# Window-attention values projected feature-major and transposed, with the first query projection freed of a wait

## The chip, the cores and the metric

The kernel runs on one core of one Trainium2 chip. The metric is the device time of one launch in microseconds (us), the median over runs. TensorE is called PE here, its weight loads PEld, VectorE DVE, ScalarE ACT, GpSimd POOL, and SP is the engine that issues the weight loads from memory.

## The reference

Two transformer-like blocks are computed one after the other on 512 latent tokens and 256 context tokens with 1024 features. The change is in the second block, which has two layers. Each layer normalises and modulates its tokens to `u`, projects them, runs three attention branches (latent-rank, differential, and local with a window), merges them with gates, and ends in a convolutional feed-forward part. The local branch is the one that changes:

```python
def window_gqa(c_lat, c_ctx, cos, sin, sink, ctx_queries):
    q, k, v = heads(*c_lat)          # 8 query heads, 2 key/value heads of 64
    cq, ck, cv = heads(*c_ctx)
    q = apply_rope(q, cos, sin)
    k = apply_rope(k, cos, sin)
    ...
        s_c = jnp.einsum('bqgrd,bkgd->bgrqk', qn, ck, ...) * scale
        s_b = jnp.einsum('bqgrd,bkgd->bgrqk', qn, kn, ...) * scale
        s_b = jnp.where(ok, s_b, NEG_INF)
        p = softmax_with_sink(jnp.concatenate([s_c, s_b], axis=-1), sink_b)
        return (jnp.einsum('bgrqk,bkgd->bqgrd', p[..., :n_ctx], cv)
                + jnp.einsum('bgrqk,bkgd->bqgrd', p[..., n_ctx:], vn))
```

Keys and values are projected from all 768 tokens, so the value matrix has 768 tokens by 128 features (two heads of 64). Layer 0 also computes the context's queries, layer 1 does not (`ctx_queries`).

## The kernel before, in words

The program is one straight line of instructions for each engine, written out by Python functions named `..._pe`, `..._act`, `..._dve`, `..._pool`. There is no loop on the chip; the order on an engine is the order in which these functions are called, and the engines meet at semaphores. Weights come as tiles of up to 128 x 2048 numbers. For each tile SP starts the load into one of four `raw` buffers once the matmuls of the tile four places earlier are done (`fill_raw`, line 177 issues it), ACT rounds it to `high` (line 203), DVE subtracts to get `low` (line 218), and PE takes both (`take`). Activations `U` are kept feature-major (features on partitions, 768 tokens along the columns) as the same kind of pair.

A product is three matmuls for each 128 features of the contraction, high by high, high by low and low by high, so 24 for a contraction of 1024 (`product`, line 269). Which operand streams through PE is chosen in two ways:

- `project`: the weights are loaded, the tokens stream. The result is feature-major, and each matmul has 512 columns (the latents) or 256 (the context).
- `token_major`: 128 tokens of `U` are loaded, the weight columns stream. The result has tokens on partitions. For n = 128 value features each matmul has 128 columns, and there are six tiles of tokens:

```python
def token_major(k, out_of, tile, c0, n, U, kcs, inc_of):
    per = 512 // n
    for i in range(0, 6, per):
        b = out_of(i // per)
        for j, t in enumerate(range(i, min(i + per, 6))):
            ins = product(k.pe, b[:, j * n:(j + 1) * n], ...)
```

PSUM is eight banks of 128 x 512 numbers `B[0]` to `B[7]`, and also four pairs of them, `W[0]` (banks 0 and 1) to `W[3]` (banks 6 and 7).

The window branch of a layer comes third, behind the merge of the differential branch. `window_keys_pe` takes the tile `wkv`, projects k with `project` into B[2] and B[3], projects v with `token_major` into B[4] and B[5], and multiplies k by the rotation matrix into B[6] (`rope_pe`, line 2740, plain float32, two records in the trace). `A.enter_pe` and `A.enter2_pe` wait until the merge before has read the banks. ACT copies k (line 2733) and v (line 2766) out. DVE and POOL finish the rotary embedding of k: POOL multiplies k by the cosines (line 2757), DVE the product by the sines (line 2747), and DVE adds them (line 2750), which gives the event `roped`.

`attention_pe` follows. It first issues the pieces of query group 0 (`window_pieces`: `q0`, the projection of 512 latents; `rq`, its rotation; `q1`, the projection of 256 context tokens, in layer 0 only). The code of `q0` holds a wait ahead of its first matmul:

```python
        if g == 0:
            pe.wait_ge("roped", (tag, "k"))
            pe.wait_ge("loaded", (tag, "v"))
```

ACT copies q out (line 3147), PE rotates it (line 3640), DVE and POOL finish it (lines 3275, 3285, 3278). Then 16 or 24 steps follow (four query groups by four or six blocks of 128 queries): scores (line 2963), mask and maximum on DVE (lines 2986, 2989, 2992), exponential on ACT (line 3007, where the first one also loads a table), normalising, transposition of the weights on PE into W[3] (line 3057), copy out on ACT (line 3064), and the product with v (line 3084). `H.ready_pe` lets the scores of a group start only when k, q and v are all loaded and k and q are rotated. Group 1 and later query pieces are issued in the gaps of these steps. `A.P` are the buffers of the exponentials; the first is written by the first exponential.

## Time and profile before

| what | value |
|---|---|
| median of 3 runs | 5345.15 us (5344.71 to 5349.12) |
| span of the profiled execution, first to last instruction | 5338.9 us |
| its own time around that span | not listed apart; the fastest run is 5.8 us longer than the span, the median 6.3 us |
| instructions | 67117 |
| busy: PE, PEld, DVE, ACT, POOL | 92%, 78%, 58%, 36%, 23% of the span |
| mean granted TensorE clock | 0.968 |
| layer 0, window branch: first k matmul to first scores | 3216.20 to 3256.63 us |
| layer 1, the same | 4691.99 to 4731.05 us |

The span is cut into its stages by the last two lines. A stage of one engine is read from the starts of its instructions, since matmuls overlap: a row's duration is longer than the distance to the next start.

### The profile page before, as it was taken

Reading aid. Unit: us, or ns where it says so; the run is one execution under the profiler, and the core shown is the slowest. Engines: PE = TensorE matmul, PEld = TensorE weight load, DVE = VectorE, ACT = ScalarE, POOL = GpSimd, SP = SyncE. Lnnn points to the kernel's source line nnn. Section 1 sums busy time; section 2 is a strip of 40 time slices with the busy share of each in tenths; the row PEclk is TensorE's granted clock in tenths of the full one; section 3 lists DMA queues with packets and bytes.
Section 4 is the critical chain, followed back from the end, with each engine's and each line's share of the span. In section 5 each row is a group of like instructions: output and inputs, shape, how many; then the busy total and the mean of one; then the engine's idle time right before and its main releaser. Section 6 shows DMA issues by size and latency. Waiting matters only on the chain.

```text
span 5338.9 us, 67117 instructions
## 1 busy us (share of the span) xinstructions
PE 4931.0 (92%) x27321; PEld 4145.3 (78%) x27321; DVE 3090.8 (58%) x5380; ACT 1910.7 (36%) x2848; POOL 1212.2 (23%) x1009
## 2 busy tenths in 40 slices
PE   7998999998899999989899999999999899889999
PEld 7887878787688878878668777778888677667787
DVE  4544456689657777776542534456666544454555
ACT  3445422235732222223342424322322443343332
POOL 1111000047644555543120002100000120021000
PEclk8999999999999999999899999999999999999999
DMA  4111124422568888875101011122322101112222
GB/s 155 49 52 57 40 80 141 158 89 111 213 247 295 306 304 307 318 283 192 52 14 68 24 40 34 44 95 101 113 103 103 50 28 65 37 52 95 87 92 74
DMA packets 157154, 636.29 MB, mean 119 GB/s; under 512 B 12352, under 2 KB 62544, under 8 KB 106288
## 3 DMA queue, kind: packets, MB, share of 16 engines
q1 hardware_dynamic: 112528, 467.97, 24.3%
q0 software_dynamic: 42240, 160.88, 8.4%
q8 instruction: 218, 3.57, 0.3%
q10 hardware_dynamic: 2080, 3.15, 0.2%
q14 instruction: 88, 0.72, 0.0%
HBM read 595.25 MB, written 36.70 MB: 118 GB/s over the span
## 4 chain that ended last, share of the span: by engine, by line
PE 64%; DVE 15%; ACT 7%; POOL 6%; issue 4%; DMA 4%; SPq 0%; DVEq 0%; ACTq 0%; POOLq 0%
PE banks L269 51%; ACT high L203 2%; DVE low L218 2%; PE banks L2958 2%; POOL ownv L2339 2%; PE banks L2963 2%; DVE ownu L2349 1%; DVE cols L2989 1%; POOL ge L2490 1%; PE banks L3057 1%; DVE oa L2275 1%; ACT P L3007 1%; PE banks L3084 1%; DMA raw<-uT_in 1%; PE banks L1022 1%
## 5 line engine op out<-in xcount | busy, mean ns | idle before, releaser
L218 DVE TENSOR_TENSOR low<-raw,high 128x2048 fp32r<-128x2048 f32 (+2 forms) x333 | 730.3, 2194 | 797.7 <-ACT high L203 775.3
L269 PE MATMUL banks<-UH,high 128*128 128x512 f32 (+2 forms) x2784 | 1016.9, 365 | 44.8 <-DVE UL L510 12.5
L269 PE MATMUL banks<-UL,high 128*128 128x512 f32 (+2 forms) x2784 | 1004.0, 361 | 0.0
L269 PE MATMUL banks<-UH,low 128*128 128x512 f32 (+2 forms) x2784 | 1002.8, 360 | 0.0
L203 ACT ACTIVATE high<-raw 128x2048 fp32r<-128x2048 f32 (+3 forms) x341 | 617.3, 1816 | 762.1 <-DMA raw<-uT_in 272.6
L269 PEld LDWEIGHTS banks<-UH,high 128*128 128x128 f32 (+1 forms) x2784 | 526.3, 189 | 146.3 <-issue 40.6
L269 PEld LDWEIGHTS banks<-UH,low 128*128 128x128 f32 (+1 forms) x2784 | 526.8, 189 | 86.3
L269 PEld LDWEIGHTS banks<-UL,high 128*128 128x128 f32 (+1 forms) x2784 | 526.6, 189 | 82.8 <-issue 0.7
L269 PE MATMUL banks<-UpH,high 128*128 128x384 f32 (+1 forms) x1152 | 404.7, 351 | 58.0 <-issue 29.5
L269 PE MATMUL banks<-UpH,low 128*128 128x384 f32 (+1 forms) x1152 | 400.7, 348 | 0.0
L269 PE MATMUL banks<-UpL,high 128*128 128x384 f32 (+1 forms) x1152 | 400.5, 348 | 0.0
L269 PE MATMUL banks<-high,actH 128*128 128x512 f32 x768 | 306.1, 399 | 29.1 <-issue 16.9
L269 PE MATMUL banks<-low,actH 128*128 128x512 f32 x768 | 303.6, 395 | 0.0
L269 PE MATMUL banks<-high,actL 128*128 128x512 f32 x768 | 303.5, 395 | 0.0
L2989 DVE TENSOR_REDUCE cols<-banks 128x1 f32<-128x768 f32 (+3 forms) x240 | 190.6, 794 | 187.1 <-PE banks L2963 107.4
L269 PEld LDWEIGHTS banks<-UpH,high 128*128 128x128 f32 x1152 | 221.3, 192 | 77.3 <-issue 70.5
L4160 POOL TENSOR_TENSOR cv<-cv 128x768 f32<-128x768 f32 (+1 forms) x44 | 68.9, 1566 | 844.3 <-DVE cv L4120 844.3
L2334 POOL DMA_INDIRECT ownu<-un_in,ownat x128 | 166.0, 1297 | 341.4 <-DVE ownu L2349 326.3
L2456 ACT ACTIVATE actH<-ge 128x384 fp32r<-128x384 f32 x128 | 67.3, 526 | 467.4 <-POOL ge L2490 463.9
L3007 ACT ACTIVATE P<-banks,cols 128x768 f32<-128x768 f32 (+3 forms) x240 | 184.7, 772 | 124.5 <-DVE cols L2994 97.3
L269 PEld LDWEIGHTS banks<-UpL,high 128*128 128x128 f32 x1152 | 221.5, 192 | 6.4
L269 PEld LDWEIGHTS banks<-UpH,low 128*128 128x128 f32 x1152 | 220.9, 192 | 5.9
(423 smaller groups left out, 9981.4 us busy)
## 6 DMA issues: line engine op xcount, KB each, us to landing
raw<-uT_in SPq DMA_DIRECT2D x64, 1024.0 KB
raw<-ev_in SPq DMA_DIRECT2D x64, 1024.0 KB
raw<-up_in SPq DMA_DIRECT2D x44, 1024.0 KB
raw<-ada_in SPq DMA_DIRECT2D x40, 1024.0 KB
gd<-stage SPq DMA_DIRECT2D x12, 2048.0 KB, 6.6
gt<-gd SPq DMA_DIRECT2D x32, 768.0 KB, 5.8
side<-ada_in SPq DMA_DIRECT2D x24, 1024.0 KB, 5.0
raw<-gate_in SPq DMA_DIRECT2D x24, 1024.0 KB
```

The lines of the kernel that those rows point to most:

```text
L203: a.e.activation(k.high[i % SPL][:, 0:w], k.raw[j % RAW][:, 0:w], ACT.Copy).then_inc(*a.inc("w_hi", j))
L218: v.e.tensor_tensor(k.low[j % RAW][:, 0:w], k.raw[j % RAW][:, 0:w], k.high[i % SPL][:, 0:w].bitcast(F32), ALU.subtract).then_inc(*v.inc("w ...
L269: ins = pe.e.matmul(out, x, y, start=start and i == 0 and j == 0, stop=stop and i == n - 1 and j == 2)
L1022: ins = pe.e.matmul(o[:, c * 64:(c + 1) * 64], w.S[:, c, x * 128:(x + 1) * 128], w.qd[:, c * 64:(c + 1) * 64], start=False, stop=(c == ord ...
L2334: g.e.indirect_dma_start(S.u[s % NUB][:], None, k.dram["un"], bass.IndirectOffsetOnAxis(S.at[:, s:s + 1], 0)).then_inc(*g.inc(f"own_u{s % ...
L2339: g.e.indirect_dma_start(S.v[s % NVB][:], None, k.dram["vn"], bass.IndirectOffsetOnAxis(S.at[:, s:s + 1], 0)).then_inc(*g.inc(f"own_v{s % ...
L2456: a.e.activation(k.acts[n % 2].h[:, i, :], k.ge[i][:], ACT.Copy).then_inc(*a.inc("act_hi", (n, i)))
L2958: ins = pe.e.matmul(k.W[1 + j][:, at:at + n], Q[lo:hi, q * 128:(q + 1) * 128], K[lo:hi, k0:k0 + n], start=True, stop=True)
L2963: ins = pe.e.matmul(k.W[1 + jj][:, at:at + n], Q[lo:hi, q * 128:(q + 1) * 128], K[lo:hi, k0:k0 + n], start=True, stop=True)
L2989: v.e.reduce_max(mx, src, AX_X).then_inc(*v.inc("largest", (tag, i, j)))
L3007: a.e.activation(A.P[i % 2][j][:, 0:width], src, ACT.Exp, bias=nb, scale=A.scale, accum_out=r).then_inc(*a.inc("exp", (tag, i, j)))
L4160: g.e.tensor_tensor(va[:, 0:w], va[:, 0:w], ga[:, 0:w], ALU.mult).then_inc(*g.inc("ffn_prod", (l, j)))
```

## The change

The function `values_act` is removed. `window_keys_pe` projects v like k, with `project`: weights loaded, tokens streaming, 512 and then 256 columns, into the same banks B[4] and B[5]. ACT copies that feature-major result to `A.vT`, which is the memory of the first exponential buffer `A.P[0][0]`. The rotation of k goes to B[0] instead of B[6]. The wait ahead of the first `q0` matmul is gone. Behind the 24 matmuls of the first `q0`, `window_values_pe` transposes vT in six blocks of 128 x 128 into W[3], and `window_values_act` copies all 768 columns to `A.v` in one instruction, behind ACT's copy of that `q0`. All this is done once in each of the two layers.

```diff
@@ window_plan
     A.plan(k)
+    A.vT = A.P[0][0]
@@ window_keys_pe
-    token_major(k, lambda i: B[4 + i], tile, 128, 128, k.U, KC,
-                lambda i: pe.inc("mm", ((tag, "v"), i), *([("tile", tile.j)] if i else [])))
+    for r, region in enumerate(BOTH):
+        project(k, B[4 + r][:, 0:region[1]], tile, KC, 128, k.U, region).then_inc(
+            *pe.inc("mm", ((tag, "vT"), r), *([("tile", tile.j)] if r else [])))
     A.enter2_pe()
-    rope_pe(k, A.k, 128, k.r64, B[6], (tag, "k"))
+    rope_pe(k, A.k, 128, k.r64, B[0], (tag, "k"))
+
+def window_values_pe(k, A):
+    pe, tag = k.pe, A.tag
+    pe.wait_ge("loaded", (tag, "vT"))
+    for t in range(6):
+        ins = pe.e.transpose(k.W[3][:, t * 128:(t + 1) * 128], A.vT[:, t * 128:(t + 1) * 128], k.ident[:])
+    ins.then_inc(*pe.inc("mm", (tag, "v")))
@@ window_keys_act
-    values_act(k, A.v, 128, (B[4], B[5]), (tag, "v"))
+    to_sbuf_act(k, (B[4], B[5]), BOTH, A.vT, 128, (tag, "vT"), (tag, "vT"))
     a.wait_ge("sinks", A.l)
+
+def window_values_act(k, A):
+    a, tag = k.act, A.tag
+    a.wait_ge("mm", (tag, "v"))
+    a.e.activation(A.v[:], k.W[3][:, 0:T].rearrange("p (t n) -> p t n", n=128), ACT.Copy).then_inc(*a.inc("loaded", (tag, "v")))
@@ window_keys_dve
-    rope_dve(k, A, A.k, 128, k.B[6], (A.tag, "k"))
+    rope_dve(k, A, A.k, 128, k.B[0], (A.tag, "k"))
@@ window_piece_pe
-        if g == 0:
-            pe.wait_ge("roped", (tag, "k"))
-            pe.wait_ge("loaded", (tag, "v"))
...
         if u == of - 1:
             ins.then_inc(*pe.inc("mm", (tag, w, g), *([("tile", A.tile.j)] if last else [])))
+            if g == 0 and p == 0:
+                window_values_pe(k, A)
@@ window_piece_act
         load_act(k, A, bank, n, 128, A.qs[g % 2][:, c0:c0 + n], ((tag, w, g), (tag, "q", g)), (tag, w, g))
+        if g == 0 and p == 0:
+            window_values_act(k, A)
```

The order moves at three places, shown for layer 0; layer 1 has the same without the `q1` piece. In the names, `high` and `low` are the two parts of a weight tile, `UH` and `UL` those of the activations, and `banks0` to `banks3` stand for W[0] to W[3].

PE, the end of the value projection, the rotation of k and the start of the first `q0`, before:

```order
L269 MATMUL banks2<-high0_57,UH_305 128x128
L269 MATMUL banks2<-low3_56,UH_305 128x128
L269 MATMUL banks2<-high0_57,UL_306 128x128
L2740 MATMUL banks3<-k_385,r64_303 128x512 [waits loaded,branch]
L269 MATMUL banks0<-UH_305,high1_58 128x512 [waits roped,loaded,w_lo,w_hi]
```

and with the change:

```order
L269 MATMUL banks2<-UH_305,high0_57 128x256
L269 MATMUL banks2<-UL_306,high0_57 128x256
L269 MATMUL banks2<-UH_305,low3_56 128x256
L2740 MATMUL banks0<-k_385,r64_303 128x512 [waits loaded,branch]
L269 MATMUL banks0<-UH_305,high1_58 128x512 [waits w_lo,w_hi]
```

The 144 value matmuls of 128 columns have become 24 of 512 and 24 of 256, the rotation of k writes banks0, and the first `q0` matmul waits for its weights only.

PE, the end of that `q0` and what follows it, before:

```order
L269 MATMUL banks0<-UH_305,low0_53 128x512
L3640 MATMUL banks1<-q_387,r64_303 128x512 [waits loaded]
L269 MATMUL banks1<-UH_305,high1_58 128x256
```

and with the change:

```order
L269 MATMUL banks0<-UH_305,low0_53 128x512
L3583 MATMUL banks3<-ident_61,P_393 128x128 [waits loaded]
L3583 MATMUL banks3<-ident_61,P_393 128x128 x5
L3645 MATMUL banks1<-q_387,r64_303 128x512 [waits loaded]
L269 MATMUL banks1<-UH_305,high1_58 128x256
```

The six transpositions stand between the projection and the rotation of q, and have a wait of their own for vT (which bears the name P here, whose memory it is).

ACT, from the copies of k to the first exponential, before:

```order
L2733 ACTIVATE k_385<-banks1 128x256 [waits mm]
L2766 ACTIVATE v_386<-banks2 128x512 [waits mm]
L2766 ACTIVATE v_386<-banks2 128x256 [waits mm]
L203 ACTIVATE high0_57<-raw2_51 128x2048 [waits w_raw2,sinks]
L3147 ACTIVATE q_387<-banks0 128x512 [waits mm]
L3147 ACTIVATE q_387<-banks1 128x256 [waits mm]
L3007 ACT_TABLE_LOAD
```

and with the change:

```order
L2733 ACTIVATE k_385<-banks1 128x256 [waits mm]
L2733 ACTIVATE P_393<-banks2 128x512 [waits mm]
L2733 ACTIVATE P_393<-banks2 128x256 [waits mm]
L203 ACTIVATE high0_57<-raw2_51 128x2048 [waits w_raw2,sinks]
L3137 ACTIVATE q_387<-banks0 128x512 [waits mm]
L3599 ACTIVATE v_386<-banks3 128x768 [waits mm]
L3137 ACTIVATE q_387<-banks1 128x256 [waits mm]
L2997 ACT_TABLE_LOAD
```

ACT has one instruction more, the copy of the transposed values, between the two copies of q. DVE and POOL keep their order.

## Rows read from the trace of the kernel before

**Rows 1.** The page: busy time of the engines, and the chain that ended last by engine

```profile
PE 4931.0 (92%) x27321; PEld 4145.3 (78%) x27321; DVE 3090.8 (58%) x5380; ACT 1910.7 (36%) x2848; POOL 1212.2 (23%) x1009
...
PE 64%; DVE 15%; ACT 7%; POOL 6%; issue 4%; DMA 4%; SPq 0%; DVEq 0%; ACTq 0%; POOLq 0%
```

**Rows 2.** The chain of waits in layer 0, 3180 to 3300: start, us, what

```profile
3240.82 0.93 PE banks L2740 x2
3241.82 1.27 POOL k L2757
...
3243.19 0.70 DVE k L2750
...
3244.13 7.39 PE banks L269 x24
...
3251.55 0.61 ACT q L3147
...
3252.20 1.12 PE banks L3640 x2
...
3256.19 0.39 ACT q L3147
3256.63 1.18 PE banks L2963 x8
```

**Rows 3.** Busy time by stretch in layer 0, columns in its first line

```profile
core 0: us, PE busy (x) PEld busy (x) DVE busy (x) ACT busy (x) POOL busy (x), PEclk, DMA share, GB/s
3216.20:3221.79 5.59, 5.59 (x26) 4.51 (x25) 1.18 (x2) 1.92 (x1) 3.96 (x5) 1.00 0.73 251
3221.79:3224.63 2.84, 2.84 (x25) 2.83 (x24) 2.24 (x2) 0.60 (x1) 0.00 (x0) 1.00 0.41 143
3224.63:3240.66 16.03, 16.03 (x146) 16.03 (x145) 0.00 (x0) 0.98 (x2) 0.00 (x0) 1.00 0.00 1
3240.66:3244.13 3.47, 1.07 (x4) 0.27 (x4) 1.64 (x3) 2.18 (x2) 1.26 (x1) 1.00 0.50 151
3244.13:3251.34 7.21, 7.21 (x24) 5.56 (x24) 1.95 (x1) 0.00 (x0) 0.00 (x0) 0.76 0.00 0
```

**Rows 4.** The same by stretch in layer 1

```profile
4700.42:4716.44 16.02, 16.02 (x146) 16.02 (x145) 0.00 (x0) 0.98 (x2) 0.00 (x0) 1.00 0.00 1
4716.44:4719.92 3.48, 1.08 (x5) 0.28 (x4) 1.65 (x3) 2.18 (x2) 1.26 (x1) 0.92 0.49 151
4719.92:4726.88 6.96, 6.96 (x24) 5.39 (x24) 1.94 (x1) 0.00 (x0) 0.00 (x0) 0.80 0.00 0
4726.88:4731.05 4.17, 1.29 (x4) 0.30 (x3) 1.39 (x2) 1.88 (x2) 1.26 (x1) 1.00 0.00 0
```

**Rows 5.** Timeline of PE in layer 0: start, us, engine, what

```profile
3267.88 0.77 PE L3057 MATMUL banks<-ident,P 128*128 128x128 f32 x5
3268.40 0.48 PE L269 MATMUL banks<-UH,high 128*128 128x512 f32 x1
```

**Rows 6.** Timeline of ACT, a copy in layer 0 and the start of layer 1's queries

```profile
3268.68 0.71 ACT L3064 ACTIVATE PT<-banks 128x640 f32<-128x640 f32 x1 [1.55 <-PE banks L3057]
...
4727.70 1.28 ACT L3007 ACT_TABLE_LOAD   x1
...
4733.52 0.69 ACT L3007 ACTIVATE P<-banks,cols 128x512 f32<-128x512 f32 x1 [4.54 <-DVE cols L2992]
```

**Rows 7.** Timeline of PE in layer 1, rotation of q and first scores

```profile
4727.73 1.12 PE L3640 MATMUL banks<-q,r 128*128 128x512 f32 x2 [0.69 <-ACT q L3147]
4731.05 1.13 PE L2963 MATMUL banks<-k,q 64*128 64x256 f32 x8 [2.19 <-DVE q L3278]
```

**Rows 8.** Busy time by stretch, from the first scores of a layer onward

```profile
3256.63:4691.99 1435.36, 1337.30 (x7749) 1096.37 (x7750) 782.07 (x1312) 482.38 (x743) 167.31 (x108) 0.98 0.20 72
4731.05:4825.00 93.95, 79.77 (x644) 57.44 (x645) 63.08 (x183) 56.73 (x137) 31.39 (x19) 1.00 0.06 18
4731.05:5338.90 607.85, 576.37 (x2766) 456.24 (x2766) 322.17 (x472) 217.46 (x307) 71.03 (x50) 0.99 0.23 79
```

More of the change, by code:

```diff
@@ L2757, in rope_pool @@
     g.e.tensor_tensor(x[0:m, 0:TX], x[0:m, 0:TX], a.C[0:m, :], ALU.mult).then_inc(*g.inc("rope_cos", key))
-def values_act(k, dst, n, banks, key):
-    a = k.act
-    per = 512 // n
-    for i, t in enumerate(range(0, 6, per)):
-        m = min(per, 6 - t)
-        a.wait_ge("mm", (key, i))
-        a.e.activation(dst[:, t:t + m, 0:n], banks[i][:, 0:m * n].rearrange("p (t n) -> p t n", n=n), ACT.Copy).then_inc(
-            *a.inc("loaded", key))
 def key_parts(kind, q):
```

## The prediction

> **What bounds the kernel now.** I read the page first: PE is busy for 92% of the span and holds 64% of the chain that ended last, no other engine more than 15% [rows 1]. So the question is what PE does, and what it waits for, between the first k matmul and the first scores of the window branch in each of the two layers. Nothing outside these two places is edited.
>
> The chain of waits in layer 0 [rows 2] passes through this place without a detour: value projection on PE, rotation of k, the cosine product on POOL, the sum on DVE, then the 24 matmuls of the first q, ACT's copy, the rotation of q, and the first scores. PE therefore stands on the path for all of it except where the chain goes to POOL and DVE, and there it stands idle.
>
> The table by stretch [rows 3, 4] gives what each step takes, from start to start:
> - the k projection in layer 0: 5.59 us for 24 matmuls of 512 columns and 2.84 for 24 of 256, together 8.43, at full clock (2.4 GHz level, 1.00 in the row);
> - the value projection: 16.03 us in layer 0 and 16.02 in layer 1 for 144 matmuls of 128 columns, PE and PEld busy all the time, full clock. That is 0.111 us for one, hardly less than the 2.84 / 24 = 0.118 of one with twice the columns;
> - the rotation of k up to the first q matmul: 3.47 and 3.48 us, of which PE works 1.07 and 1.08 and idles 2.40;
> - the first q, again 24 matmuls of 512 columns: 7.21 and 6.96 us, with a mean granted clock of 0.76 and 0.80. The clock has gone to its lower level (1.2 GHz) behind the idle 2.40 us and comes back within this q. The same 24 matmuls took 5.59 at full clock.
>
> **The change, part by part.** The sum is made on the profiled execution, whose span is 5338.9 us; the median of the runs is 5345.15, so 6.3 us lie around the span or are scatter, and the change doesn't touch them. I subtract the gain from the median.
>
> Value projection: 144 matmuls of 128 columns go, 24 of 512 and 24 of 256 come. These are the k projection's own shapes with the same activations streaming, and both regions are projected in both layers, so the price is its row, 8.43 us. Gain 16.03 - 8.43 = 7.60 in layer 0 and 16.02 - 8.43 = 7.59 in layer 1. All of it is on the path, since PE has nothing else to do there and no one holds it up: the weights of the next two tiles are split long before.
>
> The wait ahead of the first q: 2.40 us idle in each layer [rows 3, 4]. It goes whole, since the remaining condition is the split q weights, which ACT and DVE made during the merge before and at the start of k. POOL and DVE still need 0.93 (PE's rotation) + 1.27 + 0.70 and the hand-overs, from 3240.82 to 3243.89 [rows 2], but now beside the q matmuls (5.59), and only the first scores ask for the result.
>
> The clock in the first q: if PE doesn't idle, the reason for the fall is gone. 7.21 - 5.59 = 1.62 in layer 0 and 6.96 - 5.59 = 1.37 in layer 1. Bounds: nothing, if the clock falls at this place in any case, and these two differences. I take the differences, because in 3216.20 to 3240.66, with no idle time, every row has 1.00.
>
> The six transpositions: the nearest row is the same operation on the exponentials, where five start at 3267.88 and the next matmul at 3268.40 [rows 5], so 0.52 / 5 = 0.104 each and 0.62 for six. They stand where PE waits anyway: ACT's copy of q begins at 3251.55, when the projection has ended, takes 0.61, and the rotation starts at 3252.20 [rows 2]; the last q stretch ended at 3251.34 [rows 3], so 0.86 us lie there. 0.62 fits in, so the cost is 0. From below nothing; from above the row's own duration, 0.77 for five, so about 0.9 in all, would come out by less than 0.1. The ceiling is six times the whole 0.77 - 4 x 0.104 = 0.35 one after the other, 2.1 - 0.86 = 1.3 a layer. I take 0, by the distance between starts, and keep 1.3 for the range.
>
> ACT: the two copies out of B[4] and B[5] have the same sizes as those they replace, 0. The new copy of 768 columns: nearest is 0.71 us for 640 [rows 6], so about 0.85. It starts when the transpositions end, some 0.9 us behind the end of q, and is done at about 1.8. In layer 0 the next thing ACT is wanted for is the copy of q1 at 3256.19 [rows 2], 4.85 us behind that end (3251.34), so 3 us of cover. In layer 1 there is no q1: the first scores, which also wait for the values, start at 4731.05 [rows 7], 4.17 us behind 4726.88, cover 2.4; the table load behind it (1.28 us) moves from 4727.70 to about 1.1 us later, and the first exponential runs at 4733.52 [rows 6], cover more than 3. Cost 0; without that cover it would be 0.85 a layer. Also ahead of the first q copy stands the rounding of the next weight tile, which waits for the end of the value projection. It comes 7.6 us earlier like its release, and has the whole of k's rotation and q (1.07 + 5.59 = 6.66 us) to finish in.
>
> The rotation of k in B[0] instead of B[6], and DVE's sine product there: same size, 0. B[0] is waited for together with B[6], by the same condition. The buffer that vT borrows is first used by the first exponential, which comes behind the scores and so behind the values.
>
> What is late next: in layer 0 the first scores still wait for ACT's copy of q1, in layer 1 for DVE's sum of q (2.19 idle, rows 7). Both run from the rotation of q as before. Every later instruction follows this chain, and each weight tile is fetched when an earlier one is used up, so it moves along; behind the first scores the mean busy share of the DMA engines is 0.20 and 0.23 [rows 8]. The distance is kept to the end.
>
> Sum: layer 0 7.60 + 2.40 + 1.62 = 11.62; layer 1 7.59 + 2.40 + 1.37 = 11.36; together 22.98 us. 5345.15 - 22.98 = 5322.2 us. Its span would be 5315.9.
>
> The Trainium skill speaks against the price of the transpositions: the page "TensorE: Matmul & The Clock Gate", section "Part 4: PE-mode transpose", says that one of 128 x 128 costs about 275 ns inside a kernel, mostly access latency. By that six take 1.65 us, 0.79 more than the gap holds, and the sum would be 1.6 us less, 5323.8. The trace disagrees as to what the path pays: starts are 104 ns apart [rows 5].
>
> **The rivals.**
>
> *The lower clock stays in the first q.* Something else than the idle time brings it down, for instance the plain float32 rotation ahead of it. Against: the clock was 1.00 in the stretch of layer 0 that holds the rotation [rows 3]. For: in layer 1 it was already 0.92 there [rows 4]. Gain 22.98 - 2.99 = 19.99, time 5325.2.
>
> *Only the projection gains.* The wait moves instead of going: PE stands for the rotated k, or for vT, elsewhere ahead of the scores. Needed for it is a chain of over 6 us from the end of the value projection; the one of k is 3.2 (3240.82 to 3243.89 and before it 0.16), ACT's copy of vT is 0.60. Then 15.19 us are left, time 5330.0.
>
> *Given back later.* The instructions gain their 23 us, but a later stage is set by something that doesn't move, such as weight transfers, or the clock falls at new places behind waits. For: behind the first scores of layer 0 the mean clock was 0.98 for 1435 us and 0.99 for 608 [rows 8], so about 2 x 0.02 x 1435 + 2 x 0.01 x 608 = 70 us were spent at the lower level, and each such piece may come or go when all is moved by 12 to 23 us. Against: the three runs, which have the same instructions, lie within 4.4 us. So I count 4.4 us either way, and for more, down to no measurable gain, about 5339.
>
> *Slower: the clock falls at the first scores of layer 1 and stays down through the window steps.* Place: 4726.88 to 4731.05, where PE works 1.29 of 4.17 us and was granted 1.00 nonetheless [rows 4]. With the transpositions in the gap, there is less pure waiting but also hardly more real work. Price: a matmul at the lower level takes up to twice as long, so each us of work at full clock loses up to one. To turn 22.98 us of gain into 10.7 of loss (0.2%) the lower level would have to hold for work that took 34 us at full clock; the decision falls there. The first 94 us of steps hold 79.8 us of PE work at full clock [rows 8] and could lose up to that: 5402. Against: the steps of both layers already have waits of 1 to 2 us in each and recovered.
>
> The same page and section of the Trainium skill say that transpositions do not count as activity for the clock. By that rule the six would leave the gap behind q as idle as before, and this rival would be no less likely than without them. The trace of before has that gap without a fall.
>
> **How the numbers follow.** Chances: the sum with its scatter 0.88, the lower clock in q 0.04, only the projection 0.04, given back to no gain 0.03, slower 0.01. What the measurement can tell from no change is about 0.2%, 10.7 us, so 5334.5 to 5355.8. The first three cases are all faster than that: faster 0.96, same 0.03, slower 0.01. The range: 5322.2 less the 4.4 of scatter, and 1.3 for small gaps that close as well, gives 5316.5; upward it takes in the lower clock, the dear transpositions (2 x 1.3) and the case of the projection alone at 5330.0.
>
> **What the profile afterwards would show.** Right: 96 matmuls fewer in each layer; the value projection in 8.4 us; no idle time between the rotation of k and the first q, and q in 5.6 us at clock 1.00; six transpositions behind it and the rotation of q about 0.86 us behind the end of q, still released by ACT's copy; first k matmul to first scores 28.8 us instead of 40.4 in layer 0 and 27.7 instead of 39.1 in layer 1; the rest from first scores to end as long as before within a few us. Wrong: the value projection at over 9 us; a new wait of PE on ACT's vT or v; q again at 7 us without idle time ahead of it; or the stretch behind the first scores longer by more than 5 us, which would say that the gain was given back.

## The result, and the profile after

| | before | changed |
|---|---|---|
| median, us | 5347.09 (5344.71 to 5349.12, 4 runs) | 5314.55 (5308.57 to 5320.82, 4 runs) |
| ratio, 95% interval | | 0.9942 [0.9931, 0.9954] |
| profiled execution, us | | 5317.05, span 5315.7 |
| first k matmul to first scores, layer 0 / 1 | 40.43 / 39.07 | 28.82 / 27.57 |

The change makes the kernel faster, by 32.5 us in this comparison. The forecast was 5322.2 with a range from 5316.5 to 5330.0, so the median lies 2 us under its low end. The two stages came out as forecast (28.8 and 27.7). What lies between these two facts is what the experiments had to find.

The page of the changed kernel, first its size and busy times, then the chain that ended last by engine:

```profile
span 5315.7 us, 66759 instructions
...
PE 4909.2 (92%) x27141; PEld 4120.8 (78%) x27141; DVE 3092.2 (58%) x5380; ACT 1912.3 (36%) x2850; POOL 1212.0 (23%) x1009
...
PE 62%; DVE 16%; ACT 7%; POOL 6%; DMA 4%; issue 4%; SPq 0%; DVEq 0%; ACTq 0%; POOLq 0%
```

PE still bounds the kernel. Its share of the chain is 62% here and 64% in [rows 1], but other executions of the same two kernels have 62% (before) and 64% and 60% (changed), so this share tells nothing of the change. Busy time by stretch of the changed kernel, with the columns of [rows 3], the places being those of [rows 3, 4, 8]: k projection, value projection, rotation of k to rotation of q, rotation of q to first scores, then the middle; the same for layer 1, then its first scores up to the second ones, and the rest:

```profile
3219.92:3228.36 8.44, 8.44 (x51) 7.36 (x50) 3.42 (x3) 2.52 (x2) 3.95 (x5) 1.00 0.64 214
3228.36:3236.79 8.43, 8.43 (x50) 7.35 (x49) 0.00 (x0) 0.98 (x2) 0.00 (x0) 1.00 0.00 0
3236.79:3244.10 7.31, 7.28 (x35) 5.42 (x33) 3.59 (x3) 2.79 (x3) 1.30 (x1) 1.00 0.23 72
3244.10:3248.74 4.64, 3.96 (x27) 3.31 (x27) 1.39 (x2) 1.43 (x3) 1.29 (x1) 1.00 0.00 0
3248.74:4678.22 1429.48, 1331.28 (x7749) 1092.32 (x7749) 782.33 (x1312) 482.21 (x743) 167.27 (x108) 0.98 0.20 72
4678.22:4686.65 8.43, 8.43 (x50) 7.34 (x49) 3.24 (x4) 2.52 (x2) 4.67 (x6) 1.00 0.59 210
4686.65:4695.08 8.43, 8.43 (x50) 7.34 (x49) 0.00 (x0) 0.98 (x2) 0.00 (x0) 1.00 0.01 2
4695.08:4702.39 7.31, 7.28 (x35) 5.42 (x33) 3.59 (x3) 2.79 (x3) 1.31 (x1) 1.00 0.25 72
4702.39:4705.79 3.40, 1.12 (x2) 0.32 (x3) 1.39 (x2) 2.09 (x2) 1.26 (x1) 1.00 0.00 0
4705.79:4711.44 5.65, 5.65 (x21) 3.96 (x21) 3.23 (x11) 1.93 (x6) 0.00 (x0) 0.70 0.00 0
4705.79:5315.70 609.91, 579.15 (x2766) 456.69 (x2766) 322.26 (x472) 217.33 (x307) 71.01 (x50) 0.98 0.23 79
```

The value projection takes 8.43 us, the price of k's. From the rotation of k to that of q it is 7.31 us with PE busy for 7.28 of them, and the granted clock is 1.00 (the 2.4 GHz level) in both layers. One row is new: at the first scores of layer 1 the mean granted clock is 0.70 and they take 5.65 us. The same stretch of the kernel before:

```profile
4731.05:4735.63 4.58, 4.12 (x21) 2.90 (x21) 3.04 (x9) 1.89 (x6) 0.00 (x0) 1.00 0.00 0
```

So 1.07 us of the gain are given back there. At another place, the last scores of layer 0's window steps, the clock went the other way. From the scores that start 97.94 us behind the first ones to the start of the last group of scores, in the kernel before and then in the changed one:

```profile
3354.57:3375.51 20.94, 17.82 (x129) 12.05 (x129) 13.24 (x42) 11.98 (x35) 6.90 (x4) 0.77 0.00 1
```

```profile
3346.68:3365.67 18.99, 15.33 (x129) 10.63 (x129) 13.24 (x42) 12.08 (x35) 6.90 (x4) 0.91 0.01 2
```

The same instructions take 1.95 us less at a higher granted clock. It is so in every profile of the two kernels: 20.94 and 20.74 us before (0.77 and 0.84), 18.99, 18.88 and 18.72 changed (0.91 each).

The chain of waits of the changed kernel in layer 0, in order of time:

```profile
3236.95 0.86 PE banks L2740 x2
3237.81 5.60 PE banks L269 x24
3243.41 0.66 PE banks L3583 x6
3244.07 0.03 issue
3244.10 1.13 PE banks L3645 x2
3245.22 2.85 PE banks L269 x24
3248.08 0.02 issue
3248.10 0.39 ACT q L3137
3248.49 0.25 issue
3248.74 1.16 PE banks L2953 x8
```

POOL and DVE, which stood in [rows 2] with the rotation of k, are gone. The six transpositions (L3583) fill the gap between the last q matmul and the rotation of q, which begins as soon as ACT's copy of q is done. The timeline of ACT over the same stretch shows that copy, the new copy of the values, and the cover behind it:

```profile
3243.45 0.60 ACT L3137 ACTIVATE q<-banks 128x512 f32<-128x512 f32 x1 [4.27 <-PE banks L269]
3244.10 0.81 ACT L3599 ACTIVATE v<-banks 128x768 f32<-128x768 f32 x1
3248.10 0.38 ACT L3137 ACTIVATE q<-banks 128x256 f32<-128x256 f32 x1 [3.19 <-PE banks L269]
```

The copy of v takes 0.81 us, and ACT then idles 3.19 us. The spans differ by 5338.9 - 5315.7 = 23.2 us: first k matmul of layer 0 3.72 later (3216.20 to 3219.92), stage of layer 0 -11.61, middle -5.87, stage of layer 1 -11.50, rest +2.06. The stages alone give 23.11. The three others nearly cancel, and their instructions are the same in both kernels. The middle holds the 1.95 us gained at the end of layer 0's steps, and the rest the 1.07 us given back at layer 1's first scores.

### The profile page after: what moved, and what is told of

It reads as the page before. It is cut to its first block, busy times and chain, and to the rows that moved or that the text cites. A ratio compares the mean times of both kernels' runs of the same rounds, so it can differ in the third digit from the quotient of the medians.

```text
span 5315.7 us, 66759 instructions
## 1 busy us (share of the span) xinstructions
PE 4909.2 (92%) x27141; PEld 4120.8 (78%) x27141; DVE 3092.2 (58%) x5380; ACT 1912.3 (36%) x2850; POOL 1212.0 (23%) x1009
## 4 chain that ended last, share of the span: by engine, by line
PE 62%; DVE 16%; ACT 7%; POOL 6%; DMA 4%; issue 4%; SPq 0%; DVEq 0%; ACTq 0%; POOLq 0%
PE banks L269 49%; ACT high L203 2%; DVE low L218 2%; DMA raw<-uT_in 2%; PE banks L2948 2%; PE banks L2953 2%; DVE oa L2275 1%; DVE ownu L2349 1%; POOL ownv L2339 1%; POOL ge L2490 1%; PE banks L3047 1%; DVE cols L2979 1%; ACT P L2997 1%; PE banks L3074 1%; PE banks L1022 1%
## 5 line engine op out<-in xcount | busy, mean ns | idle before, releaser
L269 PE MATMUL banks<-UH,high 128*128 128x512 f32 (+2 forms) x2816 | 1028.8, 365 | 39.8 <-DVE UL L510 12.2
```

The lines of the kernel that those rows point to most:

```text
L269: ins = pe.e.matmul(out, x, y, start=start and i == 0 and j == 0, stop=stop and i == n - 1 and j == 2)
```

## The experiments

The first theory: the prediction's mechanism is whole, the stages give 23 us, and the remainder is scatter between executions that lies outside them, around a base that was taken too high. The rival: the change gains or loses elsewhere too, by way of the clock or of the buffers.

All runs in one table. Stages are from the first k matmul to the first scores; the part in brackets is from the rotation of k to that of q. early_q and early_q2 have another order, so there is nothing to put in brackets; a kernel that ran once has no ratio. Each ratio is to runs of the kernel before in the same comparison.

| run | span | ahead of layer 0's k | stage 0 | middle | stage 1 | rest | median of runs, us | ratio to the kernel before |
|---|---|---|---|---|---|---|---|---|
| kernel before | 5338.9 | 3216.20 | 40.43 (11.54) | 1435.35 | 39.07 (11.29) | 607.85 | | |
| before_again | 5332.8 | 3213.10 | 40.42 (11.53) | 1432.07 | 39.23 (11.45) | 607.98 | 5336.78 | 0.9996 [0.9983, 1.0008] |
| changed kernel | 5315.7 | 3219.92 | 28.82 (7.31) | 1429.48 | 27.57 (7.31) | 609.91 | 5314.55 | 0.9942 [0.9931, 0.9954] |
| after_again | 5317.1 | 3218.56 | 28.81 (7.30) | 1433.03 | 27.58 | 609.12 | 5316.34 | 0.9956 [0.9942, 0.9969] |
| after_third | 5309.7 | 3213.85 | 28.82 | 1430.52 | 27.58 | 608.93 | 5315.08 | 0.9953 [0.9939, 0.9966] |
| wait_only | 5332.5 | 3216.79 | 36.30 (7.35) | 1432.59 | 35.24 (7.36) | 611.58 | 5334.92 | 0.9994 [0.9985, 1.0003] |
| values_only | 5316.6 | 3213.66 | 31.25 (9.94) | 1431.59 | 30.21 (10.02) | 609.89 | 5325.38 | 0.9972 [0.9962, 0.9982] |
| values_again | 5322.6 | 3216.55 | 31.23 (9.93) | 1434.02 | 30.21 (10.02) | 610.59 | 5323.86 | |
| idle_back | 5322.3 | 3216.66 | 31.18 (9.82) | 1434.10 | 31.67 (11.39) | 608.69 | 5323.56 | |
| idle_again | 5315.7 | 3217.14 | 31.19 (9.84) | 1427.69 | 31.66 (11.37) | 608.02 | 5317.07 | |
| twelve | 5319.8 | 3220.60 | 29.17 (7.77) | 1433.45 | 27.95 (7.76) | 608.63 | 5321.14 | |
| late_turn | 5323.6 | 3221.64 | 28.81 (7.31) | 1436.25 | 27.58 (7.30) | 609.32 | 5324.97 | |
| early_q | 5317.3 | 3219.58 | 27.78 | 1432.64 | 25.18 | 612.17 | 5321.33 | 0.9962 [0.9948, 0.9975] |
| early_q2 | 5315.2 | 3219.61 | 27.78 | 1433.62 | 25.18 | 608.96 | 5312.70 | 0.9945 [0.9932, 0.9959] |

Stages repeat within 0.02 us for the same instructions and the same clock. The columns around them move by several us even between executions of one kernel (3213.10 and 3216.20 for that of before). So a stage tells apart what a median of a few runs can't.

### The same kernels once more

after_again and after_third are the changed kernel unaltered, before_again is the kernel before.

> The changed kernel once more, five rounds. Two theories for the 32.5 us between the medians, where the steps in the two window stages sum to 23.0. A (scatter): the edit is worth the 23 us of the stages and the rest is the spread of executions, so this run gives a ratio near 0.9957 (23 us less, within 4), and its profile has 28.8 and 27.6 us from the first k matmul to the first scores, with the stretches around them scattering either way. B (a further systematic gain behind the stages, by fewer falls of the clock): a ratio near 0.994 again (30 us or more less), with the stretch from the first scores of layer 0 to the first k matmul of layer 1 at 1429 to 1430 us again, where it was 1435.4.

> The kernel before against itself, five rounds, which shows what the comparison gives for no change. Theory A: ratio 1.000 within 0.0008, and a profile whose stretches outside the window stages differ by several us from the first one's (span between 5335 and 5350). Theory B: ratio 1.000 too, but the stretch between the two stages stays at 1435 within 1 us.

> The changed kernel a third time, five rounds, to see where its ratio settles. If the edit is worth what the stages show (23.1 us less up to the first scores, at most 1.1 given back in layer 1), the ratio is 0.9957 within its interval, and the stages are 28.8 and 27.6 us again while the stretches before, between and behind them move by several us. If the first comparison (0.9942) was the true one, the ratio is at or under 0.9945.

before_again has the ratio 0.9996 [0.9983, 1.0008] to the kernel before, which it is. The stages came out at 28.8 and 27.6 each time, and the middle, 1433.03 and 1430.52 in the changed kernel, was 1432.07 in before_again: theory A, the stages and scatter, holds in the main, and of theory B's gain behind the stages only the 2 us at the end of layer 0's steps are seen again. All runs together give a base that three runs could not: 58 of the kernel before, median 5340.6, from 5329.3 to 5361.1, standard deviation 5.7; 14 of the changed one, median 5315.7, from 5306.8 to 5322.8, standard deviation 4.5. The difference of the medians is 24.9, that of the means 25.0 with a 95% interval of 2.8 either way. The stages' 23.1 lie in it. With the two places where the clock changed, about 1.0 given back and 2.0 gained in the means of the profiles, some 24 us are accounted for. The interval takes the executions as independent. They come from several comparisons, and only 7 of the 54 others of the kernel before are as long as the shortest of the first four, 5344.71, so those four were probably long for a reason beyond this scatter. The four of the changed kernel beside them were not (5314.55, where all 14 have 5315.7). The later comparisons ran on chips 0, 8 and 13, that of the first isn't recorded, and the reason stays open.

Where the spread sits, busy time by stretch: from 2520.00 us to the first k matmul of layer 0, in the kernel before and then in before_again, its second profiled execution.

```profile
2520.00:3216.20 696.20, 629.11 (x3787) 502.81 (x3787) 303.04 (x578) 245.28 (x434) 90.07 (x62) 0.95 0.12 41
```

```profile
2520.00:3213.10 693.10, 625.24 (x3798) 500.96 (x3797) 303.75 (x580) 245.85 (x436) 90.07 (x62) 0.96 0.12 41
```

Nearly the same matmuls (3787 and 3798 records) take 3.10 us longer in the first, and PE is busy 3.87 us longer, at 0.95 granted instead of 0.96. So at least part of the scatter is the length of time for which the clock is down. That it is all of it isn't shown.

### One part of the change alone

wait_only takes the two waits out of the kernel before and leaves the value projection token-major:

```diff
         A.tile = view(take(k, (A.l, "wq", g // 2)), KC)
-        if g == 0:
-            pe.wait_ge("roped", (tag, "k"))
-            pe.wait_ge("loaded", (tag, "v"))
```

> Only the two waits ahead of the first q are taken out; the values stay token-major and there are no transpositions. Theory A: 2 x 2.40 us of idle time and the 2.99 us at the lower clock go, 7.8 us in all, ratio 0.9985; the value projection stays at 16.0 us, q at 5.6 in both layers. Rival, the clock falls in the first q whatever goes before: 4.8 us, and q stays at about 7. Theory B: more than 7.8, by several us.

Busy time by stretch of wait_only: rotation of k to rotation of q in layer 0 and in layer 1, then the first scores of layer 1 up to the second.

```profile
3241.26:3248.61 7.35, 6.66 (x28) 4.75 (x28) 3.59 (x3) 2.79 (x3) 1.30 (x1) 1.00 0.23 71
4710.15:4717.51 7.36, 6.67 (x29) 4.76 (x28) 3.59 (x3) 2.82 (x4) 1.30 (x1) 1.00 0.24 71
4720.92:4727.69 6.77, 6.77 (x21) 4.74 (x21) 3.37 (x11) 1.92 (x6) 0.68 (x1) 0.56 0.00 0
```

11.54 and 11.29 became 7.35 and 7.36, idle time ahead of q and slow clock both gone. The two stages are 4.13 and 3.83 shorter, together 7.96, beside 7.79 forecast (2 x 2.40 + 2.99). But the first scores of layer 1 take 6.77 us at a clock of 0.56 instead of 4.58: 2.19 us come back at once. So 5.8 us net, and the ratio, which should be 0.9989 by that, is 0.9994 [0.9985, 1.0003]: it agrees but does not tell the gain from none.

values_only keeps the waits and transposes directly behind the rotation of k (ACT's copy of the values moves forward with it, and neither stands behind q0 any longer):

```diff
     rope_pe(k, A.k, 128, k.r64, B[0], (tag, "k"))
+    window_values_pe(k, A)
...
+        if g == 0:
+            pe.wait_ge("roped", (tag, "k"))
+            pe.wait_ge("loaded", (tag, "v"))
```

> Only the projection is turned round: values in 512 and 256 columns, transposed directly behind the rotation of k, and the first q waits for the rotated k and the values as before. Theory A: 7.60 + 7.59 = 15.2 us less, ratio 0.9972; the transpositions lie inside the wait (3.47 us from the rotation to the first q stays, idle 1.7 instead of 2.4), and the clock still falls in q, 7 us. Rival, the shorter idle time no longer brings the clock down: 18.2 us. Theory B: more than 15.2 by several us.

> The same kernel as in values_only, one more look. There an idle time of 1.7 us ahead of the first q brought no fall in either layer (9.9 and 10.0 us). If idle time below 2.4 us is short enough, that is so again; if the moment decides, one of the two may be at 11.4.

The same stretches of values_only:

```profile
3230.53:3240.47 9.94, 7.52 (x34) 5.34 (x32) 3.68 (x3) 3.59 (x4) 1.26 (x1) 1.00 0.16 53
4693.37:4703.39 10.02, 7.51 (x34) 5.33 (x32) 3.68 (x3) 3.62 (x5) 1.26 (x1) 1.00 0.18 52
4706.71:4712.33 5.62, 5.62 (x20) 3.81 (x20) 3.36 (x11) 1.92 (x6) 0.00 (x0) 0.70 0.00 0
```

Stages 9.18 and 8.86 shorter, together 18.0, where the projection alone would give 15.19. The other 2.9 are the clock: PE still waits (9.94 - 7.52 = 2.42 us over the whole stretch of layer 0, of which 1.74 ahead of q, 1.83 in layer 1), but the clock stayed at 1.00. It did so again in values_again. The ratio, 0.9972 [0.9962, 0.9982], is 15.0 us of 5340, the stages less the 1.04 at the first scores being 17.0. The ratio is the one expected with the clock falling in q, and the traces show the rival instead; its interval holds both.

The two parts are therefore not additive in the clock term: either of them keeps the clock up in q, so 18.0 + 7.96 = 26.0 counts 2.9 twice, and 23.1 are had by both.

### The idle time put back into the changed kernel

```diff
         A.tile = view(take(k, (A.l, "wq", g // 2)), KC)
+        if g == 0:
+            pe.wait_ge("roped", (tag, "k"))
```

> The changed kernel with one wait put back: the first q waits for the rotated k again (not for the values). If the idle time of 2.40 us is what brings the clock down, rotation of k to rotation of q goes from 7.31 us back to about 11.4 (3.47 + about 7.1 + 0.86) in both layers, stages of 32.9 and 31.7 us. The rival, that the 16 us of 128-column matmuls ahead of it had their part in the fall: the idle time alone comes back, 9.9 us at clock 1.00, stages of 31.4 and 30.2. Where the clock falls in q of layer 1, it should not fall again at the first scores of that layer.

> The same kernel as in idle_back, one more look at the clock. There the same 2.40 us of idle time cost a fall in layer 1 and none in layer 0. If the place in the program decides, it is the same again: 9.8 us from the rotation of k to that of q in layer 0, 11.4 in layer 1. If the moment decides, at least one of the two can be otherwise.

Busy time by stretch of idle_back: the first 3.47 us from the rotation of k, then up to the rotation of q, in layer 0 and in layer 1. The first q matmul starts 3.31 us behind the rotation in both layers, after 2.29 us of idle time, so the first row of each pair ends with 0.16 us of q.

```profile
3233.53:3237.00 3.47, 1.18 (x5) 0.38 (x4) 1.69 (x3) 2.18 (x2) 1.26 (x1) 1.00 0.40 151
3237.00:3243.35 6.35, 6.32 (x30) 4.96 (x30) 1.90 (x1) 0.60 (x1) 0.00 (x0) 1.00 0.00 0
4698.81:4702.28 3.47, 1.18 (x5) 0.38 (x4) 1.70 (x3) 2.18 (x2) 1.26 (x1) 1.00 0.49 151
4702.28:4710.20 7.92, 7.89 (x31) 6.13 (x30) 1.89 (x1) 0.60 (x1) 0.00 (x0) 0.78 0.00 0
```

The whole stretch of idle_again in the two layers:

```profile
3234.01:3243.85 9.84, 7.52 (x35) 5.34 (x33) 3.59 (x3) 2.78 (x3) 1.26 (x1) 1.00 0.16 53
4692.90:4704.27 11.37, 9.05 (x34) 6.50 (x32) 3.59 (x3) 2.78 (x3) 1.26 (x1) 0.85 0.15 46
```

The idle time of some 2.3 us costs itself in both layers. In layer 1 the clock falls, and the second row has 7.92 instead of 6.35 us; in layer 0, behind the same instructions and the same idle time, it doesn't. The second execution gives the same split, so neither the expectation nor its rival came out whole. No run without the idle time had a fall in q (twelve places: two layers of six profiles), so it seems to be needed; it does not suffice, and which place falls is set by something that repeats from run to run. The prediction's "if PE doesn't idle, the reason for the fall is gone" holds; its converse does not. The rival named above, that the 128-column matmuls ahead have a part in the fall, isn't settled: the kernel before, which has them, fell in all four places, idle_back and idle_again, which don't, in two of four.

### The price of the transpositions

twelve makes the six transpositions twice:

```diff
-    for t in range(6):
+    for t in (0, 1, 2, 3, 4, 5, 0, 1, 2, 3, 4, 5):
```

> The changed kernel with each of the six transpositions of the values issued twice (same result). By the distance between starts, 0.104 us each, six more cost 0.62 us: 7.31 becomes 7.9 us from the rotation of k to that of q, in both layers. If each cost 0.27 us on the path, as its own duration has it, 12 would take 3.3 us and the stretch would be 9.9.

```profile
3237.47:3245.24 7.77, 7.77 (x41) 6.15 (x40) 3.59 (x3) 2.79 (x3) 1.31 (x1) 1.00 0.20 67
4700.10:4707.86 7.76, 7.76 (x40) 6.14 (x39) 3.59 (x3) 2.79 (x3) 1.31 (x1) 1.00 0.22 68
```

From the rotation of k to that of q 7.77 instead of 7.31: six more cost 0.46 us. PE has no idle time left there (busy 7.77 of 7.77). The timeline of PE in layer 0 of twelve gives the distance between starts:

```profile
3243.93 1.47 PE L3583 MATMUL banks<-ident,P 128*128 128x128 f32 x12
3245.24 0.59 PE L3645 MATMUL banks<-q,r 128*128 128x512 f32 x1
```

The same in the changed kernel:

```profile
3243.25 0.82 PE L3583 MATMUL banks<-ident,P 128*128 128x128 f32 x6
3244.10 0.70 PE L3645 MATMUL banks<-q,r 128*128 128x512 f32 x1
```

Twelve take 1.31 us from their first start to the rotation of q, 0.109 each where [rows 5] gave 0.104. Six are then 0.65 of the 0.85 us that lie there in the changed kernel, which leaves 0.20, and the 0.46 are the other six less that. By the 275 ns of the Trainium skill ("TensorE: Matmul & The Clock Gate", "Part 4: PE-mode transpose") six more would be 1.65 us. The trace agrees with that figure as the duration of one (0.27 us: 1.47 less eleven times 0.109), but what the path pays is the distance between starts, 0.109.

### Where the transpositions stand in layer 1

late_turn moves them, in layer 1 only, from behind q0 to behind the rotation of q, into PE's wait ahead of the first scores:

```diff
         pe.e.matmul(bank, k.r64[:], A.qs[g % 2][:, 0:TX], start=True, stop=True).then_inc(...)
+        if g == 0 and not A.ctx_out:
+            window_values_pe(k, A)
...
-            if g == 0 and p == 0:
+            if g == 0 and p == 0 and A.ctx_out:
                 window_values_pe(k, A)
```

> In layer 1 alone the six transpositions go behind the rotation of q, into the idle time ahead of the first scores (2.28 us). The stages stay at 28.8 and 27.6 us. If it is that idle time which brings the clock down at the first scores of layer 1, a break of 1.6 us instead of 2.28 lets it stay at 1.00, and the first scores to the second take 4.6 us instead of 5.65. The rival, that transpositions do not keep the clock up: 5.65 as before.

```profile
4714.28:4718.83 4.55, 4.13 (x20) 2.94 (x21) 3.04 (x9) 2.40 (x7) 0.00 (x0) 1.00 0.00 0
```

The stages stay at 28.81 and 27.58, so this place is free as well. The first scores of layer 1 take 4.55 us at full clock, 1.10 less than in the changed kernel, as expected. But twelve, which didn't move the transpositions, had no fall there either, nor did idle_back and idle_again, whose q is slow instead. So the full clock here can't be put down to the place of the transpositions. What decides at the first scores stays open.

### A version that waits for nothing

early_q orders PE as k, q0, values of the latents, rotation of k, rotation of q0, values of the context, q1, transpositions. Each rotation then has a projection to hide behind, and v is awaited only by the first transposition of the weights instead of by the first scores:

```diff
             k.pe.wait_ge("roped", (tag, "k"))
-            k.pe.wait_ge("loaded", (tag, "v"))
...
+    project(k, B[1], A.tile, KC, 0, k.U, XR).then_inc(*pe.inc("mm", (tag, "q0", 0)))
+    project(k, B[4], tile, KC, 128, k.U, XR).then_inc(*pe.inc("mm", ((tag, "vT"), 0)))
     rope_pe(k, A.k, 128, k.r64, B[0], (tag, "k"))
+    pe.wait_ge("loaded", (tag, "q0", 0))
+    pe.e.matmul(B[2], k.r64[:], A.qs[0][:, 0:TX], start=True, stop=True).then_inc(*pe.inc("mm", (tag, "rope", "rq", 0)))
+    project(k, B[5][:, 0:TC], tile, KC, 128, k.U, CR).then_inc(...)
...
-    if g % 2 == 0 and p == 0:
+    if g < 3 and p == 0:
         turn_act(k)
```

> A new order for the window stage: k, first q, values of the latents, rotations of k and q, values of the context, then (layer 0) q of the context, then the transpositions; the scores no longer wait for the values, the first transposition of weights does; the next weight tile is rounded with the second query group. The projections cover the rotary embeddings, and ACT's copies are covered too. Expected 27.9 us instead of 28.8 in layer 0 and 25.2 instead of 27.6 in layer 1, and no fall of the clock at the first scores of layer 1 (1.1 us): 4.4 us less than the changed kernel, ratio to the kernel before 0.9948. Rival: the copies of vT or the rounding moved into the steps show up as waits, and the stages gain but the rest loses the same.

The stages are 27.78 and 25.18 us, PE busy for 27.78 and 25.15 of them: nothing is waited for any more, 3.4 us less than in the changed kernel. The ratio is 0.9962 [0.9948, 0.9975] where 0.9948 was expected: no better than the changed kernel. The expectation's rival came about. The rounding of the next weight tile (`turn_act`, the last lines of the diff) now falls among the steps. Timelines of early_q in layer 1, ACT and then PE:

```profile
4715.65 1.91 ACT L203 ACTIVATE high<-raw 128x2048 fp32r<-128x2048 f32 x1
4717.45 0.59 ACT L3139 ACTIVATE q<-banks 128x512 f32<-128x512 f32 x1
```

```profile
4723.91 1.37 PE L2953 MATMUL banks<-k,q 64*128 64x256 f32 x8 [4.01 <-ACT P L2997]
```

The rounding of 1.91 us, and 2.29 us of DVE behind it, stand ahead of the exponentials and maxima of a step; PE idles 4.01 us ahead of the next scores; in layer 0 it idles 2.62 us ahead of a rotation of q whose copy stands behind the rounding. The fifth scores start 26.52 us (layer 0) and 24.0 us (layer 1) behind the first ones, where it is 22.52 and 21.78 in the changed kernel: 4.0 and 2.2 us lost for the 3.4 gained.

early_q2 puts the rounding back: on ACT behind the copy of the feature-major values, on DVE behind the first maxima, and the copy of v behind the first exponentials.

> The new order of early_q with its cost taken away: there the rounding of the next weight tile (1.92 us on ACT, 2.29 on DVE), moved into the steps, made the fourth step of both layers late by 1.9 and 3.3 us. Here ACT rounds as soon as the value projection has released the tile and copies the values behind the first exponentials; DVE does its half behind the first maxima. Expected stages of 27.8 and 25.2 us as in early_q, and steps that lose at most 1 us in each layer: 3 us less than the changed kernel from k to the end of the steps. By the rounds, a ratio between 0.994 and 0.9965, not to be told from the changed kernel's 0.9956.

Stages again 27.78 and 25.18. The steps of layer 0 start 0, 5.66, 11.06, 18.09 and 23.64 us behind the first scores, in the changed kernel 0, 4.54, 9.94, 16.98 and 22.52: one delay of 1.1 us, once. The timeline of ACT in layer 0 of early_q2 shows it, the same table load in the changed kernel below it:

```profile
3249.98 1.28 ACT L2999 ACT_TABLE_LOAD   x1 [2.75 <-DVE cols L2982]
```

```profile
3248.50 1.28 ACT L2997 ACT_TABLE_LOAD   x1
```

In the changed kernel the table is loaded ahead of the first exponential's wait, in idle time. In early_q2 it stands behind that wait, on the path. In layer 1 the table load stands behind the wait as well, and the fifth step starts at 21.76, as in the changed kernel, which loses as much by its clock. Net 3.4 - 1.1 = 2.3 us better by the stages and steps, 5312.7 us (5302.53 to 5316.45, 5 runs), ratio 0.9945 [0.9932, 0.9959]. That can't be told from the changed kernel's 0.9942, 0.9956 and 0.9953. With the table load back ahead of the wait 1.1 more might be had; it wasn't tried.

## Why the prediction was right, and where it was wrong

- **Value projection**, 7.60 and 7.59: from the first k matmul to the rotation of k 24.46 became 16.87 and 16.86 in the two layers, so 7.59 and 7.60. Right.
- **The wait**, 2.40 each, gone: the row with 3.47 us, of which PE works 1.07, has no counterpart. **The clock in q**, 1.62 and 1.37: 24 matmuls in 5.60 us (chain of the changed kernel), clock 1.00 in both layers. Together with the transpositions, 11.54 to 7.31 and 11.29 to 7.31, 4.23 and 3.98 where 4.02 and 3.77 were summed. Right within 0.21: from the rotation of k to the first transposition 6.46 us (3236.79 to 3243.25) where the sum has 1.07 + 5.59 = 6.66, since the first q matmul starts while the rotation still runs, and the gap behind q is 0.85 as before. The experiments add that either part alone, no wait or the turned projection with 1.7 us of idle time left, kept the clock up in q.
- **Transpositions**, 0: hidden behind ACT's copy of q, and with 0.20 to spare. The price was 0.109 each and not 0.104. Right.
- **ACT**, 0: the copy of v took 0.81 (0.85 estimated), with 3.19 us idle behind it. Right.
- **What is late next**: as foreseen, ACT's copy of q1 in layer 0 and DVE's sum of q in layer 1. Rotation of q to scores 4.64 and 3.40, where it was 4.43 and 3.32, so 0.21 and 0.08 more, where nothing was forecast.
- **The clock behind the stage.** The prediction had the distance kept to the end, and had a fall at layer 1's first scores only as the rival on the other side, which stays down through the steps. The place was right and the extent not: the fall came in all three profiles, ended before the second scores, and cost 1.07, 1.07 and 0.94 us. (The first profile had one more, of 1.2 us, late in layer 1's steps, which the other two don't have.) Nor did the sum have the 2.0 us gained at the end of layer 0's steps. Two clock terms that it put at nothing are thus about -1.0 and +2.0; that they partly cancel is luck.
- **The base.** This is the step that failed: "5345.15, so 6.3 us lie around the span or are scatter ... I subtract the gain from the median", and with it "the three runs ... lie within 4.4 us. So I count 4.4 us either way". In every execution whose span is listed 1.3 us lie around it (5317.05 and 5315.7; 5334.07 and 5332.8). So the profiled execution of before took about 5338.9 + 1.3 = 5340.2, 5 us under the median of three and right at the median of 58, 5340.6. The three runs, 5344.71 to 5349.12, were all in the upper part, and their 4.4 us was not the spread of the kernel: the 58 lie over 31.8 us. From 5340.2, the sum of 22.98 gives 5317.2, beside 5315.7 for the median of 14 and 5314.55 for that of the first four. The range laid the same way around that base, 5311.5 to 5325.0, would hold both. Of the 6.5 us between the forecast, 5322.2, and the median of 14, 4.6 are the base and 1.9 the gain, within its interval. The 4.4 us of scatter was too narrow as well. Why the first four runs of before were all long stays open.

None of the rivals came as written: the clock did not stay low in q, the wait did not move to another place, and the gain was given back only by about 1 us. The first comparison showed 32.5 us because its four runs of before had a median 6.5 us over that of all 58, and its four of the changed kernel one 1.1 us under that of all 14; the stages have 23.1 and the pooled runs 24.9.

**Open.** Why the clock falls in one place and not in another behind the same idle time (q of layer 1 in idle_back, not of layer 0; first scores of layer 1 in the changed kernel, not in twelve or late_turn). The Trainium skill ("TensorE: Matmul & The Clock Gate", "Part 4: PE-mode transpose") says that a transposition doesn't count as busy time of PE in the way a matmul does, by which six more could not have kept the clock up at the first scores; twelve has 1.00 there and the changed kernel 0.70, but late_turn has 1.00 too with six, so these runs neither bear the rule out nor refute it. The starting positions in time, the work ahead and the length of the wait all differ a little between these, and no run here varied one of them alone.

## What to carry to other kernels

Take the base for a sum from the profiled execution plus what lies around its span, and set the range by more than the spread of three runs: three runs lay within 4.4 us here and 58 over 31.8. To prove a change of a few us in one of 5300, compare the stretch from one named matmul to another in two traces, which repeated within 0.02 us where the clock was the same (39.07 and 39.23 where it wasn't), and let runs in their dozens, from more than one comparison, confirm it. Then look for places outside the stretch where the clock changed in every profile. When a wait is taken out, look at the next gap as well: the clock may fall there instead, and a step that was moved carries its roundings and table loads with it.

## What the runs showed of the hardware

- The same kernel on one core: 5329 to 5361 us over 58 runs, with the same instructions; between two traces 3.1 us of the difference lie in one stretch with a lower mean granted clock (0.95 and 0.96 over 696 and 693 us).
- Float32 transpositions of 128 x 128 in a row start 0.109 us apart, though one lasts 0.27 us (twelve).
- Idle time of about 2.3 us ahead of the first q: clock 0.78 behind it in layer 1 and 1.00 in layer 0, the same split in both executions.
- The mean granted clock at the first scores of layer 1 went with what came ahead: 1.00 in the kernel before, idle_back, twelve and late_turn, 0.70 in the changed kernel and values_only, 0.56 in wait_only. At the last scores of layer 0's window steps it was 0.77 and 0.84 in the kernel before and 0.91 in three profiles of the changed one.
- The table load of 1.28 us stood ahead of the first exponential's wait in one order of ACT's work and behind it in another, and was on the path in the second.
